# One third of the second table's rows added by GpSimd, all rows scaled by ScalarE, none added by VectorE

## What is computed

```python
def block(xb):                       # xb: 128 tokens x 1024
    q = (xb @ w_peer_q).reshape(PEER_BLOCK, PEER_HEADS, 2, D_KEY // 2)
    s = jnp.einsum('thpd,hpnd->thpn', q, peer_sub_keys)
    ...                              # top 16 of each head: experts e, gates g (8 x 16 = 128 per token)
    act = jax.nn.gelu(jnp.einsum('td,thkd->thk', xb, peer_u[e]))
    return jnp.einsum('thk,thkd->td', g * act, peer_v[e])
```

## Time and profile before

| | us |
|---|---|
| median of 3 runs | 2189.94 (2189.35 to 2194.55) |
| profiled execution | 2195.0 |
| its span, first to last instruction | 2193.2 |

### The profile page before, as it was taken

One profiled execution on the slowest core, in us unless ns is written; L12 is line 12 of the kernel. 1 busy time (PEld: TensorE's weight loads), 2 busy tenths in 40 slices (PEclk: granted clock), 3 DMA queues, 4 the chain that ended last, 5 costly groups with the idle time before them and its releaser, 6 DMA issues.

```text
span 2193.2 us, 27671 instructions
## 1 busy us (share of the span) xinstructions
PE 1738.6 (79%) x8934; PEld 1272.8 (58%) x8934; DVE 1601.9 (73%) x3603; ACT 1273.8 (58%) x2840; POOL 634.3 (29%) x657
## 2 busy tenths in 40 slices
PE   7996799776896897997896896985786796775776
PEld 3554656635665666765665664764665565554654
DVE  2455685486699789768886787887789889768444
ACT  1233343237477654477898688894555555546665
POOL 1000000034334333333433333342333433343331
PEclk9998598786898886797997898896897897886666
DMA  7000300179999999989999999996999999999997
GB/s 274 17 20 13 87 1 30 49 294 420 416 411 398 393 366 343 404 328 386 403 419 364 418 409 372 419 410 255 420 363 391 390 374 392 313 418 372 420 419 295
DMA packets 108353, 695.70 MB, mean 317 GB/s; under 512 B 16688, under 2 KB 19120, under 8 KB 31408
## 3 DMA queue, kind: packets, MB, share of 16 engines
q0 software_dynamic: 95376, 674.29, 76.7%
q1 hardware_dynamic: 12832, 19.65, 3.0%
HBM read 690.14 MB, written 3.76 MB: 316 GB/s over the span
## 4 chain that ended last, share of the span: by engine, by line
PE 38%; DVE 28%; DMA 12%; ACT 9%; ACTq 4%; DVEq 4%; issue 4%; POOL 1%; another core or an unknown queue 0%; POOLq 0%
DMA region<-in_peer_rows,region 11%; DVE region L1696 9%; PE ps L2035 6%; PE ps L2229 6%; DVE xall L1704 4%; DVEq L1103 4%; ACTq L1087 4%; PE ps L1985 3%; PE ps L1720 3%; ACT region L1091 2%; PE ps L2052 2%; ACT region L1088 1%; PE ps L2017 1%; PE ps L1888 1%; ACT region L1010 1%
## 5 line engine op out<-in xcount | busy, mean ns | idle before, releaser
L689 POOL DMA_INDIRECT region<-in_peer_rows,region x576 | 567.2, 985 | 1421.5 <-PE ps L2229 752.9
L1696 DVE SCALAR_TENSOR_TENSOR region<-region,h_now 128x1024 f32<-128x1024 f32 x576 | 695.8, 1216 | 203.4 <-DMA region<-in_peer_rows,region 191.1
L2229 PE MATMUL ps<-ident,region 128*128 128x128 f32 x3352 | 567.8, 327 | 248.0 <-ACT region L1091 225.1
L2229 PEld LDWEIGHTS ps<-ident,region 128*128 128x128 f32 x3352 | 472.7, 170 | 353.1 <-ACT region L1091 297.6
L1091 ACT ACTIVATE region<-region 128x1024 f32<-128x1024 f32 x419 | 481.3, 1149 | 34.5 <-issue 0.8
L1086 ACT ACTIVATE region<-region 128x1 f32<-128x1 f32 x576 | 113.2, 196 | 330.3 <-DVE region L1696 322.6
L2035 PE MATMUL ps<-w_uk_s,region 128*128 128x512 f32 x544 | 282.1, 644 | 5.9 <-ACT region L953 5.9
L1704 DVE SCALAR_TENSOR_TENSOR xall<-region,xall 128x1024 f32<-128x1024 f32 x157 | 201.8, 1285 | 78.1 <-ACT region L1088 64.0
L1088 ACT ACTIVATE region<-region 128x1 f32<-128x1 f32 x576 | 169.7, 295 | 40.1 <-issue 0.7
L2035 PEld LDWEIGHTS ps<-w_uk_s,region 128*128 128x128 f32 x544 | 102.0, 209 | 82.8 <-issue 74.9
L953 ACT ACTIVATE region<-ps 128x512 f32<-128x512 f32 x136 | 79.6, 586 | 78.2 <-PE ps L2035 76.1
(11 more groups left out here) (394 smaller groups left out, 2689.5 us busy)
## 6 DMA issues: line engine op xcount, KB each, us to landing
region<-in_w_peer_q POOLq DMA_DIRECT2D x16, 1024.0 KB
region<-in_peer_rows,region POOLq DMA_INDIRECT x576
...
```

The costliest lines, as they stand in the source:

```text
L689: pool.indirect_dma_start(ring[r][:], None, a["peer_rows"], bass.IndirectOffsetOnAxis(ap=experts[:, t, n:n + 1], axis=0)).then_inc(landed[ ...
L1696: v.scalar_tensor_tensor(ring[r][:, 0:D], ring[r][:, 0:D], 1.0, h_now[:], ALU.mult, ALU.mult, accum_out=acts[:, t % 2, n:n + 1]).then_inc( ...
L2229: last = te.matmul(ps[6 + c // 4][:, (c % 4) * P:(c % 4 + 1) * P], ring[r][:, D + c * P:D + (c + 1) * P], ident[:], is_transpose=True, sta ...
```

## The change

on_dve, SHARES and HEAD go. on_pool(m) names the rows that POOL adds: rows 0 to 5 of tile 0, then every third row of each prompt tile (n divisible by 3), and n = 1 of tiles 1 to 3: 179 rows. The other 397 are PE's. ACT scales all 576 rows, and `v_scaled` counts all of them. POOL adds a row in add_row, a tensor_tensor of xall and the scaled half, just before the fetch that refills the row's place, and counts `v_pooled`; that fetch waits for the add. DVE adds no rows; y_add of a prompt tile now waits for POOL's adds of the tile. y_turn(1) on PE also waits for `sel_kept`.

```diff
-        SHARES = [(0, MIXED_AT, 1, 1), (38, 54, 3, 4), (100, 160, 2, 3), (167, 184, 1, 2), (258, 275, 1, 2), (362, 480, 3, 5), (480, 496, 1, 2)]
-        HEAD = 4
-        def on_dve(m):
...
+        POOL_EVERY = 3
+        def on_pool(m):
+            return m < SEQ and (m < MIXED_AT or m % P % POOL_EVERY == 0 or m >= P and m % P == 1)
...
+            def add_row(m):
+                t, n = tile_of(m)
+                r = place_of["e", t, n]
+                pool.wait_ge(S["v_scaled"], m + 1)
+                hold(pool, S["v_pooled"], pool_rows(m))
+                nc.gpsimd.tensor_tensor(xall[:, t, :], xall[:, t, :], ring[r][:, D:W], ALU.add).then_inc(S["v_pooled"], 1)
+
             for f, what in enumerate(fetched):
+                if f >= NRING:
+                    kind, t, n = fetched[f - NRING]
+                    if kind == "e" and on_pool(P * t + n):
+                        add_row(P * t + n)
...
-                    elif on_dve(x):
-                        pool.wait_ge(S["v_mixed"], x - pe_rows(x) + 1)
+                    elif on_pool(x):
+                        pool.wait_ge(S["v_pooled"], pool_rows(x) + 1)
...
-                    sc(weight, act_, ACT.Copy, scale=gates[:, t, n:n + 1]).then_inc(S["wts"], 1)
-                    if not on_dve(m):
-                        act.drain()
-                        sc(ring[r][:, D:W], ring[r][:, D:W], ACT.Copy, scale=weight).then_inc(S["v_scaled"], 1)
+                    sc(weight, act_, ACT.Copy, scale=gates[:, t, n:n + 1])
+                    act.drain()
+                    sc(ring[r][:, D:W], ring[r][:, D:W], ACT.Copy, scale=weight).then_inc(S["v_scaled"], 1)
...
-                settle()
+                if t < NTILE - 1:
+                    dve.wait_ge(S["v_pooled"], pool_rows(P * (t + 1)))
...
-                if 0 <= m < NCOLS and on_dve(m):
-                    t, n = tile_of(m)
-                    r = place_of["e", t, n]
-                    dve.wait_ge(S["wts"], m + 1)
-                    settle()
-                    v.scalar_tensor_tensor(xall[:, t, :], ring[r][:, D:W], wts[:, t % 2, n:n + 1], xall[:, t, :], ALU.mult, ALU.add).then_inc(S["v_mixed"], 1)
...
+                    pe.wait_ge(S["sel_kept"], 2)
```

20 lines of the change are left out of this document (7 added, 13 removed).

## The result

| | before | after |
|---|---|---|
| median, us | 2189.20 (2181.46 to 2194.55, 7 runs) | 2206.72 (2204.39 to 2217.73, 7 runs) |
| ratio after / before | | 1.0097, 95% interval 1.0074 to 1.0120 |
| profiled execution, us (its span) | 2195.0 (2193.2) | 2217.73 (2215.6) |

The forecast was 2178 and faster. The time lies inside the range that was given, but the sign is wrong. The profiled execution of after is 11 us above its median, that of before 6 us above its own, so a difference of 5 us between the two profiles may be scatter.

The account below looks back on a forecast made before the run. Limits differ by stretch: transfers (floor 417 GB/s), DVE in 1529 to 1921, PE in crowded ones. Terms -22 + 4 + 3 - 8 + 8 + 3 = -12 us gave 2183 profiled, 2178 as median; range 2135 to 2225.

Parts of the forecast that it names:

- I cost the adds at nothing in the steady stretches: Steady stretches: POOL's 2.2 us adds cost nothing, hidden by its 1421.5 us of idle time in front of fetches.
- The crossing of 3.4 us: POOL's queue: only adds of 3.4 us or more make three fetches and one add outlast three rows' transfers, 7.47 us.
- the three stretches bound by the transfers: Steps 54 to 100, 184 to 258, 275 to 351: PE loses 64 rows; at most 21 us to gain, -8 taken.
- 1529 to 1921: Trace time in us, steps 361 to 480: DVE holds the transfers back; gain between 0 and 34, -22 taken.
- the fourth rival: The attentions' chain sets the pace, 1529 to 1921 keeps its 392 us: 2200 us in all, chance 0.14.
- The PE rival: PE takes DVE's place as bound in steps 100 to 160 and 361 to 480: +31, 2221 us, chance 0.16.
- The POOL rival: POOL becomes the bound from adds of 3.4 us on; at 4.4 us +62, near 2240 us, chance 0.11.
- DVE and POOL in each other's way: DVE's work stands still during POOL's adds, no gain in 1529 to 1921: 2200 us, chance 0.07.
- ACT at nothing: ACT scales 157 rows more at 1149 ns, 180 us in all, costed at nothing under cover of the transfers.
- First rows, +8: Rows 0 to 5, added by POOL between refills at 3.7 us each: +8 us, from +2 to +14.

Follow-up runs that it names:

- e1: After, but POOL's add covers 16 of the row's 1024 columns: 2178.09 us, ratio 0.9954.
- e5: After, but POOL fills the used-up row with zeros (two fills, 1.93 us) in place of the add: 2196.88 us, ratio 1.0046.
- e9: After, but POOL makes longer fills (2.36 us) in place of the add: 2200.78 us, ratio 1.0060.
- e10: After, but PE takes the rows of steps 54 to 100 (past each tile's first four), 184 to 256 and 275 to 361: 2201.48 us, ratio 1.0062.
- e6: After, but POOL adds the 157 rows that DVE added in before, over 16 columns only: 2176.23 us, ratio 0.9956.
- e7: Before, but from row 361 on ACT scales and POOL adds the 79 rows that were DVE's: 2171.48 us, ratio 0.9937.
- e2: After, but POOL adds the 157 rows that DVE added in before, the other 419 on PE: 2189.37 us, ratio 1.0020.
- e4: Before, but ACT also scales DVE's 157 rows and DVE adds them after that: 2228.76 us, ratio 1.0182.
- e8: After, but DVE adds rows 0 to 5 as in before: 2207.18 us, ratio 1.0116.
- e13: After, but outside steps 38 to 54, 100 to 184 and 256 to 275 POOL adds the rows DVE added in before: 2193.44 us, ratio 1.0054.
- e14: After, but in steps 38 to 54, 100 to 184 and 256 to 275 POOL adds the rows DVE added in before: 2211.52 us, ratio 1.0129.

## Why the prediction was wrong

- **"I cost the adds at nothing in the steady stretches; what hides them is POOL's idle time."** This is the step that failed, and with it the sentence it rests on, "POOL reads the row right after ACT's scaling ... so the place is not refilled later than now". The duration was right (2.2 us forecast, 2.38 measured), and so was the count. The crossing of 3.4 us compared POOL's throughput over three rows with the transfers': 6.2 us for 7.5. Throughput wasn't what this in-order queue of refills lived by. The earlier trace rows already held the hint: 752.9 of the 1421.5 us were waits for PE, that is, POOL stood at a refill and could not go on to an add. The add comes after that wait, in the median 1.6 us after the scaling, and ahead of the next refill, 4.2 us after it, 2.0 with the short add. So an add makes a refill later by up to its own length; the ring of eight rows takes most of that up, but not all. e1, e5 and e9 show the price: 29 us for 179 adds of 2.38 us, 19 and 23 for fills of 1.93 and 2.36 us, none of which the sum had.
- **"the three stretches bound by the transfers ... I take -8."** It was +17.9 in the profiles. Taking 64 rows off PE gave nothing here, even with short adds (549.2 us for 539.8 before, e1), so PE's rows didn't set the pace, and the rows that were taken off went to the queue of the refills. Without adds in these stretches 8 us come back by the ratio, 5 by the medians (e10). Even with short adds steps 54 to 100 take 132.9 us, as in after, where the old split takes 127.7 (e6): a part of the loss there isn't the adds' length. The clock fell there as well (0.88 to 0.77). It goes with the rows that leave PE and not with the adds' length: 0.81 in e1, 0.89 in e6, 0.85 in e10, where the rows are PE's again. What the lower clock costs, no run separates.
- **"1529 to 1921 ... I take -22."** The mechanism was right and the size was not. DVE fell from 330.5 to 255.0 us (239 forecast) and left the head of the chain of waits: it is led now by

```profile
by line: PE ps L2036 9.9%; DMA region<-in_peer_rows,region 9.6%; PE ps L2231 8.9%; issue 7.2%; ACTq L1095 7.0%; PE ps L2157 4.3%; PE ps L2129 4.3%; DVE region L1704 4.2%; ACT region L1098 3.2%; PE ps L2053 2.6%; DVEq L1110 2.2%; DVE region 
```

  where the earlier trace rows had DVE's add and dot product with 28%. But the time is 386 us, 6 less. With the old split it is 13 less (e7, e2), with short adds as well 18 (e6). The full gain of 34 to 37 was in none of the runs: with little of DVE's and POOL's adds left 374 us remain, 19 above the transfers, and PE is busy 81% of them. What holds these 19 us is not shown. The chain of the attentions between PE, ACT and DVE, the fourth rival, is one candidate; the transfers themselves, which also carry the cache pages and whose engines are busy 99% at 398 GB/s in e6, are another.
- **The PE rival (0.16)** gave 378 us for steps 361 to 480 and 217 for steps 100 to 160. It is refuted as the main cause: the whole new split costs 2 us when the adds are short, and steps 100 to 160 took 194.8. The granted clock did rise in steps 100 to 160 (0.79 to 0.86; 0.81 and 0.76 in e2 and e6, where PE has its old rows), as argued. In steps 361 to 480 it rose to 0.90, but to 0.88 in e2 and e7 with PE's old rows as well: most of that rise comes with DVE's relief.
- **The POOL rival (0.11)** had the right engine and the wrong condition. It asked for adds above 3.4 us; adds of 2.38 us do it in part, their effect on DVE included, at 0.08 us of time for each us of work added (29 us for 179 x 2.12 us = 379 us).
- **DVE and POOL in each other's way (0.07)** is real and was rated too low: 63 us of standstill, 21 of which the long fills cause as well, and some 6 us of the time (e9 against after), the weakest number here, since the intervals overlap. The price named for it, 2200 with all adds of the stretch lost, had the wrong reason: the dot product isn't caught.
- **ACT at nothing**: not contradicted on POOL's path (steps 361 to 480 get faster in e2 and e6 with all rows scaled), and it would have cost 40 us on DVE's (e4). "ACT holds 83 to 88% in 1010 to 1480" leaves out the middle stretch, where it is 71% (39.5 of 56 us).
- **First rows, +8**: +6.2 measured. Each refill took 3.6 us (3.7 forecast), and the extra ISA instruction cost nothing that shows: the first add starts at 468.09, 0.1 us after the eighth fetch has ended. From the start of the eighth fetch to the end of the fourteenth 23.8 us were forecast, and 22.8 are measured in the timeline of after:

```profile
467.05 0.94 POOL L697 DMA_INDIRECT region<-in_peer_rows,region  x1 [0.30 <-issue]
468.09 2.37 POOL L657 TENSOR_TENSOR xall<-xall,region 128x1024 f32<-128x1024 f32 x1
...
488.93 0.95 POOL L697 DMA_INDIRECT region<-in_peer_rows,region  x1 [0.27 <-POOL xall L657]
489.90 2.37 POOL L657 TENSOR_TENSOR xall<-xall,region 128x1024 f32<-128x1024 f32 x1
492.54 0.95 POOL L697 DMA_INDIRECT region<-in_peer_rows,region  x1 [0.27 <-POOL xall L657]
```

  A seventh add, of row 6, stands behind it, which the prediction left out. Yet taking six of the adds away brought no gain that can be seen (e8), so it is doubtful that the term belonged into a sum of times to the end.

What stays open: how the 17 us between e2 and after divide between DVE's standstill, the refills behind an add in the stretches bound by the transfers, PE's rows and the lower clock. The profiles put most of it into the three stretches bound by the transfers and steps 361 to 480; e13 and e14 agree that it lies outside the crowded steps.
